# Second model, first layer: head pairs in the latent attention, its rotations moved ahead

## The chip, the cores and the metric

The kernel runs on one core of one Trainium2 chip. The metric is the device time of one execution in microseconds (us), the median of several runs; less is better.

## What is computed

The reference runs two models of two layers each on the same core: a hybrid mixer of four parts, and a second model that takes two token streams of 256 tokens (latent and context, 1024 channels) through a feed-forward part, a mixer and another feed-forward part in each layer, with a layer norm behind each. The change touches only the mixer of the second model's first layer, `even_mixer`. It runs a gated linear attention (GLA, four heads) and a latent attention (MLA, four heads: 128 channels without rotation, 64 rotated, values of 128), side by side on the same input:

```python
def apply_rope(x, cos, sin):
    x2 = x.reshape(*x.shape[:-1], -1, 2).astype(jnp.float32)
    x0, x1 = x2[..., 0], x2[..., 1]
    out = jnp.stack([x0 * cos - x1 * sin, x0 * sin + x1 * cos], axis=-1)
    return out.reshape(x.shape).astype(x.dtype)

def dense_attention(q, k, v, scale):
    ...
    def block(qi):
        s = jnp.einsum('bqhd,bkhd->bhqk', qi, k).astype(jnp.float32) * scale
        p = jax.nn.softmax(s, axis=-1).astype(v.dtype)
        return jnp.einsum('bhqk,bkhd->bqhd', p, v)
    ...

# inside even_mixer
    gla_l = gla_out(o_lf + flip(o_lb), r_l, gla_norm_g)
    q_l = jnp.concatenate([qn_l, apply_rope(qr_l, cos[None, :, None], sin[None, :, None])], axis=-1)
    kr_l_rot = apply_rope(kr_l, cos[None], sin[None])
    k_l = jnp.concatenate([kn_l, jnp.broadcast_to(kr_l_rot[:, :, None], rope_shape)], axis=-1)
    ...
    mla_l = dense_attention(q_l, k_all, v_all, MLA_SCALE).reshape(B, S, -1)
    yl = jnp.concatenate([gla_l, mla_l], axis=-1) @ w_out
    ...
    mla_c = dense_attention(q_c, k_c, v_c, MLA_SCALE).reshape(B, Tc, -1)
```

The latent queries see all 512 keys, the context queries the 256 context keys. Only the latent half of queries and keys is rotated; all four heads share one rotated key.

## The kernel before

Everything is written by hand: one instruction stream for each engine, with named semaphores (`on[...]`) between them. Weights come as slabs over SP's DMA queue into `raw`, a ring of four. ACT copies a slab to a rounded high part and DVE subtracts it from the slab to get the low part (`split_hi` L336, `split_lo` L340, called one slab ahead by `act_ahead` and `dve_ahead`); a product is then three matmuls, high by high, high by low and low by high (`dense` and `product` L375, `token_major` L417). The activations are split in the same way into `xh` and `xl`. An output bank pair is free again when `drained[...]` of its parity says so, and `last_pair` waits for both.

**The mixer's stages.** In `pe_even`, `act_even` and `dve_even`, slabs k = 0 to 8 of the input projection make the GLA queries and keys, the low-rank gate input and the rotated key (`LK`, chunk 0 and chunk 1), the compressed queries and keys `CQ`, the values and the gate `RS`. Beside them DVE and ACT work out the gates of the GLA's two directions. Then the GLA itself runs, and its output stands in `OA`. Seven small slabs follow (`uq` 0 to 2 and `ukv` 0 to 3): they make `QN` and `QR` (queries without and with rotation), `KN` (keys) and `VM` (values), token major. Beside these DVE normalises `OA` (L1347), multiplies it by `RS` (L1350), ACT copies it to `xh` (L1070) and DVE subtracts for `xl` (L1352).

**The rotation.** When the last slab is drained, PE permutes the latent half of `QR` (L1195) and of the key `LK` (L1196), two fp32 matmuls with a constant. DVE runs six operations (L1358 to L1363) that multiply by cosine and sine and add. `qk2_ready` then lets PE begin the attention.

**The attention.** `pe_attend`, `act_attend` and `dve_attend` go over `MLA_UNITS`: 16 units, one head and one block of 128 queries each. The 8 latent units have 512 keys, the 8 context units 256. For a unit PE computes the scores into one bank, as the sum of a product over 128 channels (`KN`, `QN`) and one over 64 (`LK`, `QR`), both L897; the 64 channels of an even head lie in partitions 0 to 63, those of an odd head in 64 to 127. DVE finds the negated maximum (L978) and scales it (L981), ACT takes the exponential with its sum (L941), DVE divides (L996, L999), PE transposes (L908), ACT copies back to `PTM` (L958) and PE multiplies by the values (L921). Two units are one head's output, which ACT and DVE split (L948, L989). Scores and probabilities have two buffers. PE's own order is what sets the pace:

```python
for u in range(len(units)):
    turn(u)
    if u + 2 < len(units):
        score(u + 2)
    if u:
        output(u - 1)
```

When all eight outputs are split, `pe_out` begins the output projection.

**The other layer's attention.** The second layer has a neighbourhood attention of 16 heads (`pe_pairs`, `act_pairs`, `dve_pairs`), which already goes by pairs of heads, one from each half of the partitions: four score banks, both scores of a pair next to each other (L1400, 64 channels each, 512 keys), then the transposes (L1409) and the products with the values (L1419). DVE has one operation more for each head there, a bias that is added to the scores.

Of the kernel before, what the change touches and what calls it, by code (L numbers as in the profile page):

```python
# [199 lines left out]
def build(nc, a):  # L200
# [8 lines left out]
    with ctx:  # L209
# [48 lines left out]
        def vcol(name, i, n=1):  # L258
# [28 lines left out]
        ml = phase([("c2_", [P, C2_N]), ("PR", [P, 2, 512]), ("K_", [P, 2, 2 * T]), ("LK_", [P, 2, 2 * T]),  # L287
                    ("PTM", [P, 2, 512]), ("V_", [P, 2, 512]), ("CQ_", [P, 4, 2 * T]),
# [202 lines left out]
        def segments(u):  # L491
# [8 lines left out]
                    soft_max exp_done p_ready pt_ready pt_copied pv_done o_taken pool_in pool_out var_ready root_done mixh_done x6_ready half_out x_centred row_ready row_out ln_all ln_sixth v_act cq_rstd cq_rows gq_rstd gq_rows qk_ready qb_ready n_max n_soft n_exp n_norm n_tr n_copy n_pv n_hi n_lo ctx_hi ctx_lo  # L500
                    mixl_done gates_e kc_ready rms_sum sc_ready mod_final xm_hi xm_lo x_scaled gate_act h_hi h_lo ln_sq ln_in
                    ln_sum z_out z_in z_ln ge_in ge_done kq_ready kd_t kdt_done att_out att_masked u_out s_ready og_out oa_done
                    gq_sum gq_sq mg_hi mg_ready cq_sq cq_sum cq_ready cq_hi cq_lo qk2_ready rm_out c2_in c3_in fmax fsoft fexp
                    fnorm ftr fcopy fpv fhi flo qkv_ready""".split()
# [67 lines left out]
        MLA_UNITS = [(h, blk, 0) for h in range(4) for blk in range(2)] + [(h, blk, 1) for h in range(4) for blk in range(2)]  # L572
# [307 lines left out]
        def unit_keys(units, u):  # L880
            return (0, 2 * T) if units[u][2] == 0 else (T, 2 * T)

        def groups(units, na):

            step = 4 if na else 2
            return {g * step + step - 1: g for g in range(len(units) // step)}

        def pe_attend(pe, units, na, f0, g0, q_ap, k_ap, v_ap, pr, ptm):

            def score(u):  # L890
                h, blk, ctx_ = units[u]
                k0, k1 = unit_keys(units, u)
                if f0 + u >= 2 and u >= 2:
                    pe.wait_ge(on["fexp"], f0 + u - 1)
                pairs = q_ap(h, ctx_ * T + blk * P, k0, k1)
                for n, (q, k) in enumerate(pairs):
                    mm = pe.matmul(PS[:, u % 2, 0:k1 - k0], q, k, start=n == 0, stop=n == len(pairs) - 1)  # L897
                mm.then_inc(on["fmax"], 1)
            score(0)
            score(1)  # L900

            def turn(u):
                k0, k1 = unit_keys(units, u)
                pe.wait_ge(on["fnorm"], f0 + u + 1)
                if u >= 2:
                    pe.wait_ge(on["fcopy"], f0 + u - 1)
                for kt in range((k1 - k0) // P):
                    mm = pe.transpose(PS[:, 2 + u % 2, kt * P:(kt + 1) * P], pr[:, u % 2, kt * P:(kt + 1) * P], ident)  # L908
                mm.then_inc(on["ftr"], 1)

            def output(u):
                h, blk, ctx_ = units[u]
                k0, k1 = unit_keys(units, u)
                pe.wait_ge(on["fcopy"], f0 + u + 1)
                g = u // (4 if na else 2)
                if g >= 2 and u % (4 if na else 2) == 0:
                    pe.wait_ge(on["flo"], g0 + g - 1)
                rows = slice((h % 2) * HD, (h % 2) * HD + HD) if na else slice(0, P)
                nk = (k1 - k0) // P
                for kt in range(nk):  # L920
                    mm = pe.matmul(PS[rows, 4 + g % 2, blk * P:(blk + 1) * P], v_ap(h, k0 // P + kt),  # L921
                                   ptm[:, u % 2, kt * P:(kt + 1) * P], start=kt == 0, stop=kt == nk - 1)
                mm.then_inc(on["fpv"], 1)
# [1482 lines left out]
```

## Time and profile before

| | |
|---|---|
| median of 3 runs | 2261.88 us (2260.73 to 2262.16) |
| the profiled execution: time, span | 2258.81 us, 2257.0 us |
| PE, DVE, ACT, POOL busy, share of the span | 94%, 62%, 33%, 6% |
| mean granted TensorE clock | 0.958 |
| PE, first matmul of the rotation | at 959.38 us |
| PE, first matmul of the attention | at 965.46 us |
| PE, first matmul of the output projection | at 1017.95 us |

Times are those of the span, which begins with the first instruction. The granted clock is 1 at 2.4 GHz and 0.5 at 1.2 GHz. An fp32 matmul stands in the trace as two records, so "x2" is one such matmul of the program, and the time from one row's start to the next row's start tells what it took.

### The profile page before, as it was taken

The numbers are of one execution on the slowest core, as the hardware profiler recorded it, in microseconds if no ns is written. First come the engines' busy times: TensorE is split into PE (matmuls) and PEld (weight loads), VectorE is DVE, ScalarE is ACT, GpSimd is POOL, SyncE is SP. The second block draws the span as 40 slices with busy tenths as digits, with TensorE's granted clock in tenths as the row PEclk, the third lists the DMA queues.
The fourth block names the chain that finished last, engine by engine and source line by source line (L and its number), as shares of the span: only waits on it lengthen the run. The fifth ranks groups of instructions, "written<-read, shape, count | busy, mean of one in ns | idle before, by whom it ended". The sixth has DMA issues, their size and how long they took to land. (4 is left out here: it accounts for less than half of the span.)

```text
span 2257.0 us, 28660 instructions
## 1 busy us (share of the span) xinstructions
PE 2113.5 (94%) x11984; PEld 1782.5 (79%) x11984; DVE 1392.5 (62%) x2005; ACT 745.8 (33%) x929; POOL 138.7 (6%) x127
## 2 busy tenths in 40 slices
PE   7979987999999899798999999899999989898997
PEld 6958966887887788647887887788888879778997
DVE  5775686586676556554676686555455455576555
ACT  3444345321121444233421222431122242355332
POOL 0400120000001100002000000100000200010001
PEclk9988988999999999889999999999999999998999
DMA  5553463455453310202355553242442333114552
GB/s 208 180 168 112 170 206 112 149 169 202 163 191 114 106 64 19 81 18 94 126 190 180 171 186 120 90 177 92 169 157 100 108 144 130 55 41 137 174 177 89
DMA packets 69209, 301.29 MB, mean 133 GB/s; under 512 B 6112, under 2 KB 24160, under 8 KB 49120
## 3 DMA queue, kind: packets, MB, share of 16 engines
q1 hardware_dynamic: 65712, 289.20, 37.2%
q10 hardware_dynamic: 3376, 10.37, 1.3%
q8 instruction: 89, 1.46, 0.3%
q14 instruction: 32, 0.26, 0.0%
HBM read 298.50 MB, written 1.05 MB: 133 GB/s over the span
## 5 line engine op out<-in xcount | busy, mean ns | idle before, releaser
L375 PE MATMUL PS<-xh,wh 128*128 128x512 f32 (+1 forms) x3740 | 1034.5, 351 | 23.6 <-DVE xl L2089 13.2
L375 PEld LDWEIGHTS PS<-xh,wh 128*128 128x128 f32 x3740 | 679.6, 190 | 119.3 <-issue 11.3
L375 PE MATMUL PS<-xl,wh 128*128 128x512 f32 (+1 forms) x2134 | 730.1, 342 | 0.0
L336 ACT ACTIVATE wh<-raw 128x2048 fp32r<-128x2048 f32 (+3 forms) x228 | 390.2, 1713 | 341.6 <-PE PS L375 238.7
L340 DVE TENSOR_TENSOR wh<-raw,wh 128x2048 fp32r<-128x2048 f32 (+3 forms) x188 | 388.4, 2066 | 131.6 <-ACT wh L336 131.2
L375 PEld LDWEIGHTS PS<-xl,wh 128*128 128x128 f32 x2134 | 407.9, 191 | 45.4
L375 PE MATMUL PS<-HH,wh 128*128 128x512 f32 (+1 forms) x1408 | 399.9, 368 | 6.6 <-DVE wh L340 6.6
L375 PEld LDWEIGHTS PS<-HH,wh 128*128 128x128 f32 x1408 | 253.7, 188 | 56.2 <-DVE wh L340 8.8
L832 DVE CUSTOM_DVE_ANT_0 NRM<-SQ,CBR 128x1024 f32<-128x1024 f32 x240 | 283.8, 1219 | 5.8
L375 PE MATMUL PS<-HL,wh 128*128 128x512 f32 (+1 forms) x704 | 258.5, 367 | 0.0
L774 ACT ACTIVATE SI<-PS 128x512 f32<-128x512 f32 (+1 forms) x88 | 48.1, 546 | 607.1 <-PE PS L375 575.4
L846 DVE TENSOR_TENSOR HF<-SI,PS 128x512 f32<-128x512 f32 (+1 forms) x88 | 54.6, 621 | 262.5 <-ACT SI L774 262.5
L661 DVE SCALAR_TENSOR_TENSOR X<-PS,mod,X 128x256 f32<-128x256 f32 x136 | 60.0, 479 | 154.3 <-PE PS L375 153.8
L375 PEld LDWEIGHTS PS<-HL,wh 128*128 128x128 f32 x704 | 132.6, 188 | 24.9
L375 PE MATMUL PS<-xh,rest 128*128 128x256 f32 x528 | 151.7, 287 | 0.0
L405 PE MATMUL PS<-xh,wh 128*128 128x512 f32 (+1 forms) x384 | 123.5, 403 | 26.4 <-DVE xl L628 26.4
L340 DVE TENSOR_TENSOR rest<-raw,wh 128x2048 fp32r<-128x2048 f32 (+2 forms) x40 | 89.4, 2241 | 38.4 <-ACT wh L336 37.8
L405 PEld LDWEIGHTS PS<-xh,wh 128*128 128x128 f32 x384 | 77.6, 209 | 43.8 <-issue 21.9
L689 POOL TENSOR_TENSOR NRM<-X 128x512 f32<-128x512 f32 (+1 forms) x6 | 6.7, 1113 | 1670.4 <-DVE X L661 1670.4
L375 PEld LDWEIGHTS PS<-xh,rest 128*128 128x128 f32 x528 | 103.8, 197 | 0.0
L678 ACT ACTIVATE SQ<-X 128x512 f32<-128x512 f32 (+2 forms) x42 | 25.7, 612 | 218.5 <-DVE X L661 218.5
L417 PE MATMUL PS<-wh,xh 128*128 128x256 f32 x400 | 75.6, 292 | 4.6 <-DVE wh L340 4.6
(322 smaller groups left out, 1935.6 us busy)
## 6 DMA issues: line engine op xcount, KB each, us to landing
raw<-ffi_dram SPq DMA_DIRECT2D x88, 1024.0 KB, 5.0
SQ<-adat_dram SPq DMA_DIRECT2D x120, 512.0 KB, 4.0
raw<-ffo_dram SPq DMA_DIRECT2D x64, 704.0 KB, 4.3
raw<-layer_dram SPq DMA_DIRECT2D x36, 1024.0 KB, 4.9
lent<-layer_dram SPq DMA_DIRECT2D x14, 1024.0 KB, 8.1
raw<-odd_dram SPq DMA_DIRECT2D x12, 1024.0 KB, 4.8
raw<-even_dram SPq DMA_DIRECT2D x9, 1024.0 KB, 4.9
raw<-eout_dram SPq DMA_DIRECT2D x4, 1024.0 KB, 4.8
```

The source lines that it names most:

```text
L336: act.activation(high(i)[:, 0:n], raw[:, i.slot, 0:n], ACT.Copy).then_inc(hi_done, 1)
L340: eng.tensor_tensor(low(i)[:, 0:n], raw[:, i.slot, 0:n], high(i)[:, 0:n].bitcast(F32), ALU.subtract).then_inc(lo_done[who], 1)
L375: m = pe.matmul(out, w[rows, o:o + P], x, start=n == 0 and j == 0, stop=n == len(tiles) - 1 and j == 2)
L405: m = pe.matmul(PS[:, 2 * j.par + c, 0:n], w[:, o:o + P], x[:, k, 0:n], start=k == 0 and g == 0, stop=k == KT - 1 and g == 2)
L417: m = pe.matmul(out, x[:, krow + k, tt * P:(tt + 1) * P], w[:, k * n:(k + 1) * n], start=k == 0 and j == 0, stop=k == kts - 1 and j == 2)
L661: mm = dve.scalar_tensor_tensor(out=xk, in0=PS[:, bank, br * T:(br + 1) * T], scalar=g, in1=xk, op0=ALU.mult, op1=ALU.add)
L678: act.activation(SQ[:, part, 0:n], X[:, part, 0:n], ACT.Square).then_inc(on["ln_sq"], 1)
L689: ins = pool.tensor_tensor(NRM[:, j, 0:n], src[:, 0, 0:n] if k == 1 else NRM[:, j, 0:n], src[:, k, 0:n], ALU.add)
L774: act.activation(SI[:, i.par, 0:n], PS[:, 2 * i.par, 0:n], ACT.Silu).then_inc(on["gate_act"], 1)
L832: mm = dve.tensor_tensor_reduce(out=NRM[:, 2 * br:2 * br + 2, :].rearrange("p a n -> p (a n)"), in0=ADA[:, n % CHUNK_RING, :], in1=CBR[:, ...
L846: dve.tensor_tensor(hf, SI[:, i.par, 0:n], PS[:, 2 * i.par + 1, 0:n], ALU.mult)\
```

## The change

**Head pairs.** `pe_mla`, `act_mla` and `dve_mla` take the place of the three functions of the attention. They go over 8 pairs: two heads, one block of 128 queries; four latent pairs with 512 keys, then four context pairs with 256. A pair has both products over 128 channels and then both over 64 channels, the latter from the two halves of the partitions and into two banks. Scores and probabilities have four buffers, and a pair of heads has one output bank, which ACT and DVE split in one operation each.

**Rotations.** The permutation of the key goes behind slab k = 3 of the input projection and its three DVE operations to k = 4. The permutation of the queries goes behind `ukv` slab 1, once DVE has normalised `OA` (new semaphore `gq_read`, since both use bank 4), and its three DVE operations come in slab k = 5 of the seven small ones, ahead of the splitting of the next slab.

**The rest of the GLA output.** Multiplying by `RS`, copying to `xh` and subtracting for `xl`, three operations of 2048 columns, become four of 512 columns each, put between the pairs.

```diff
-        ml = phase([("c2_", [P, C2_N]), ("PR", [P, 2, 512]), ("K_", [P, 2, 2 * T]), ("LK_", [P, 2, 2 * T]),
-                    ("PTM", [P, 2, 512]), ("V_", [P, 2, 512]), ("CQ_", [P, 4, 2 * T]),
+        ml = phase([("c2_", [P, C2_N]), ("PR", [P, 4, 512]), ("LK_", [P, 2, 2 * T]),
+                    ("PTM", [P, 4, 512]), ("CQ_", [P, 4, 2 * T]),
...
+        MLA_PAIRS = [(hp, blk, c) for c in range(2) for hp in range(2) for blk in range(2)]
...
+        def pe_mla(pe):
+            def scores(w):
...
+                if w >= 2:
+                    pe.wait_ge(on["m_exp"], 2 * w - 2)
+                for e in range(2):
+                    pe.matmul(PS[:, 2 * (w % 2) + e, 0:k1 - k0], ml["QN"][:, 2 * hp + e, q], ml["KN"][:, 2 * hp + e, k0:k1], start=True, stop=False)
+                for e in range(2):
+                    r = slice(e * HD, e * HD + HD)
+                    pe.matmul(PS[:, 2 * (w % 2) + e, 0:k1 - k0], ml["QR"][r, hp, q], ev["LK"][r, 1, k0:k1], start=False, stop=True)\
+                        .then_inc(on["m_max"], 1)
+            def turn(w):
...
+                for e in range(2):
+                    pe.wait_ge(on["m_norm"], 2 * w + e + 1)
+                    if w:
+                        pe.wait_ge(on["m_copy"], 2 * w + e - 1)
...
+            for w in range(len(MLA_PAIRS)):
+                turn(w)
+                if w + 2 < len(MLA_PAIRS):
+                    scores(w + 2)
+                if w:
+                    output(w - 1)
...
+        def act_mla(act):
...
+            for w in range(n):
+                for e in range(2):
+                    if w + 1 < n:
+                        exp(2 * w + 2 + e)
+                    copy(2 * w + e)
+                if 2 <= w < 6:
+                    act.wait_ge(on["mg_ready"], w - 1)
+                    act.activation(xh[:, w - 2, :], ev["OA"][:, w - 2, :], ACT.Copy).then_inc(on["mg_hi"], 1)
+                if w and w % 2 == 0:
+                    hi(w // 2 - 1)
...
+        def dve_mla(dve, ch):
...
+            for w in range(n):
+                for e in range(2):
+                    normal(2 * w + e)
+                    if w + 1 < n:
+                        maxima(2 * w + 2 + e)
+                if w < 4:
+                    dve.tensor_tensor(ev["OA"][:, w, :], ev["OA"][:, w, :], ev["RS"][:, w, :], ALU.mult).then_inc(on["mg_ready"], 1)
+                else:
+                    dve.wait_ge(on["mg_hi"], w - 3)
+                    dve.tensor_tensor(xl[:, w - 4, :], ev["OA"][:, w - 4, :], xh[:, w - 4, :].bitcast(F32), ALU.subtract)\
+                        .then_inc(on["mg_lo"], 1)
...
@@ pe_even, slab k == 3 of the input projection
                     gate_inputs(0)
+                    pe.matmul(PS[:, 7, 0:T], cst("permM"), ev["LK"][:, 1, 0:T], start=True, stop=True).then_inc(on["rk_out"], 1)
@@ pe_even, ukv
+                if k == 1:
+                    pe.wait_ge(on["gq_read"], 1)
+                    pe.matmul(PS[:, 4, :], cst("permM"), ml["QR"][:, :, 0:T], start=True, stop=True).then_inc(on["rm_out"], 1)
             last_pair(pe, Idx(START["ukv"] + 3))
-            pe.wait_ge(on["mg_ready"], 1)
-            pe.matmul(PS[:, 4, :], cst("permM"), ml["QR"][:, :, 0:T], start=True, stop=True)
-            pe.matmul(PS[:, 5, 0:T], cst("permM"), ev["LK"][:, 1, 0:T], start=True, stop=True).then_inc(on["rm_out"], 1)
             pe.wait_ge(on["qk2_ready"], 1)
...
-            pe.wait_ge(on["flo"], 8)
+            pe_mla(pe)
+            pe.wait_ge(on["m_lo"], 4)
+            pe.wait_ge(on["mg_lo"], 4)
             pe_out(pe, 1)
```

The moves on two engines, as lists of their instructions. First PE at the attention's first units, before. `KN`, `QN` is the product over 128 channels, `LK`, `QR` the one over 64, `const`, `PR` a transpose, `PTM`, `VM` the product with the values:

```order
L1195 MATMUL PS<-QR,const 128x512
L1196 MATMUL PS<-LK,const 128x256
L897 MATMUL PS<-KN,QN 128x512
L897 MATMUL PS<-LK,QR 128x512
L897 MATMUL PS<-KN,QN 128x512
L897 MATMUL PS<-LK,QR 128x512
L908 MATMUL PS<-const,PR 128x128 x4
```

The same place with the change:

```order
L891 MATMUL PS<-KN,QN 128x512 x2
L894 MATMUL PS<-LK,QR 128x512 x2
L891 MATMUL PS<-KN,QN 128x512 x2
L894 MATMUL PS<-LK,QR 128x512 x2
L904 MATMUL PS<-const,PR 128x128 x8
```

Both products of a kind now stand next to each other, with eight transposes behind them in place of four, and the permutations (L1195, L1196) are gone from this place.

DVE between the keys' second copy and the first maximum, before. `wh` is a slab's low part, `VM` the values' copy out of their banks, `c` the table of cosines and sines:

```order
L1332 COPY KN<-PS 128x1024
L1350 TENSOR_TENSOR OA<-OA,RS 128x2048
L340 TENSOR_TENSOR wh<-raw,wh 128x256
L1334 COPY VM<-PS 128x4x256
L340 TENSOR_TENSOR wh<-raw,wh 128x2048
L1334 COPY VM<-PS 128x4x256
L1352 TENSOR_TENSOR xl<-OA,xh 128x2048
L1358 TENSOR_TENSOR PR<-PS,c_94 128x512
L1359 TENSOR_TENSOR PR<-PS,c_94 128x256
L1360 TENSOR_TENSOR QR<-QR,c_94 128x2x256
L1361 TENSOR_TENSOR LK<-LK,c_94 128x256
L1362 TENSOR_TENSOR QR<-QR,PR 128x2x256
```

With the change:

```order
L1337 COPY KN<-PS 128x1024
L340 TENSOR_TENSOR wh<-raw,wh 128x256
L1339 COPY VM<-PS 128x4x256
L1358 TENSOR_TENSOR PR<-PS,c_94 128x512
L1359 TENSOR_TENSOR QR<-QR,c_94 128x2x256
L1360 TENSOR_TENSOR QR<-QR,PR 128x2x256
L340 TENSOR_TENSOR wh<-raw,wh 128x2048
L1339 COPY VM<-PS 128x4x256
L975 TENSOR_REDUCE tiny<-PS 128x1
```

The three operations on the queries now stand between the two copies to `VM`, ahead of the big slab's low part; those on `LK` and the two on `OA` are gone from here.

## Rows read from the trace of the kernel before

**Rows 1.** Windows, busy time by engine; the first line names the columns
```profile
core 0: us, PE busy (x) PEld busy (x) DVE busy (x) ACT busy (x) POOL busy (x), PEclk, DMA share, GB/s
818.00:842.00 24.00, 24.00 (x135) 20.11 (x134) 14.11 (x15) 11.60 (x8) 0.00 (x0) 1.00 0.08 23
921.00:926.00 5.00, 4.78 (x11) 3.81 (x12) 1.12 (x2) 2.64 (x2) 0.00 (x0) 0.50 0.02 3
950.00:965.00 15.00, 6.35 (x21) 4.09 (x19) 11.75 (x12) 4.99 (x3) 0.00 (x0) 0.51 0.57 205
965.00:981.00 16.00, 15.54 (x23) 5.02 (x23) 4.88 (x14) 3.31 (x8) 0.00 (x0) 0.50 0.00 0
983.50:997.30 13.80, 13.80 (x67) 7.74 (x66) 6.83 (x18) 5.66 (x15) 0.00 (x0) 1.00 0.00 0
1004.50:1012.20 7.70, 7.70 (x42) 5.05 (x41) 5.05 (x18) 3.91 (x14) 0.00 (x0) 1.00 0.02 3
```

**Rows 2.** Timeline of PE: start, us, line, tiles, count [idle before <-releaser]
```profile
948.80 0.50 PE L417 MATMUL PS<-wh,xh 128*128 128x256 f32 x2 [2.67 <-DVE wh L340]
...
959.38 2.05 PE L1195 MATMUL PS<-QR,const 128*128 128x512 f32 x2 [3.99 <-issue]
961.22 1.06 PE L1196 MATMUL PS<-LK,const 128*128 128x256 f32 x2
965.46 2.07 PE L897 MATMUL PS<-KN,QN 128*128 128x512 f32 x2 [3.17 <-DVE LK L1363]
```

**Rows 3.** Timeline, DVE, second gate, last projections and rotation
```profile
853.46 0.16 DVE L1277 TENSOR_SCALAR tiny<-PS 128x4 f32<-128x4 f32 x1 [6.90 <-PE PS L1115]
...
945.95 2.34 DVE L1347 SCALAR_TENSOR_TENSOR OA<-OA,vec,PS 128x2048 f32<-128x2048 f32 x1
...
949.80 2.28 DVE L1350 TENSOR_TENSOR OA<-OA,RS 128x2048 f32<-128x2048 f32 x1
...
955.86 2.29 DVE L340 TENSOR_TENSOR wh<-raw,wh 128x2048 fp32r<-128x2048 f32 x1 [2.31 <-ACT wh L336]
958.06 1.22 DVE L1334 COPY VM<-PS 128x1024 f32<-128x1024 f32 x1
```

**Rows 4.** Timeline, PE, one unit of 512 keys and the next one's start
```profile
983.48 1.02 PE L897 MATMUL PS<-KN,QN 128*128 128x512 f32 x2
984.43 1.12 PE L897 MATMUL PS<-LK,QR 64*128 64x512 f32 x2
985.49 1.16 PE L921 MATMUL PS<-PTM,VM 128*128 128x128 f32 x8
...
986.92 1.02 PE L897 MATMUL PS<-KN,QN 128*128 128x512 f32 x2
```

**Rows 5.** Timeline, PE, one unit of 256 keys and the next one's start
```profile
1006.47 0.60 PE L897 MATMUL PS<-KN,QN 128*128 128x256 f32 x2
1007.00 0.70 PE L897 MATMUL PS<-LK,QR 64*128 64x256 f32 x2
1007.62 0.71 PE L921 MATMUL PS<-PTM,VM 128*128 128x128 f32 x4
...
1008.39 0.60 PE L897 MATMUL PS<-KN,QN 128*128 128x256 f32 x2
```

**Rows 6.** Timeline, PE, attention end and first output matmul
```profile
1015.40 0.44 PE L908 MATMUL PS<-const,PR 128*128 128x128 f32 x2 [0.64 <-DVE PR L999]
...
1017.95 0.50 PE L375 MATMUL PS<-xh,wh 128*128 128x512 f32 x1 [0.93 <-DVE xl L989]
```

**Rows 7.** Timeline, PE, the other layer's attention, its first pairs
```profile
1954.01 1.11 PE L1409 MATMUL PS<-const,NP 128*128 128x128 f32 x4 [1.00 <-DVE NP L1477]
...
1958.97 0.66 PE L1409 MATMUL PS<-const,NP 128*128 128x128 f32 x4 [1.18 <-DVE NP L1477]
1959.55 1.13 PE L1400 MATMUL PS<-NK,NQ 64*128 64x512 f32 x4
1960.61 1.09 PE L1419 MATMUL PS<-NPT,NV 128*64 128x128 f32 x16
```

More of the change, by code:

```diff
@@ L877, in dve_ffn @@
             post_norm(dve, ch, m)
[L880 to L918, printed above, removed]
-                nk = (k1 - k0) // P
[L920 to L923, printed above, removed]
-            for u in range(len(units)):
-                turn(u)
-                if u + 2 < len(units):
-                    score(u + 2)
-                if u:
-                    output(u - 1)
-            output(len(units) - 1)
@@ new lines, in dve_mla, with maxima, normal @@
+        def dve_mla(dve, ch):
+            n = len(MLA_PAIRS)
+            def maxima(v):
+                k0, k1 = mla_keys(v // 2)
+                dve.wait_ge(on["m_max"], v + 1)
+                nm = tiny[:, v % 4:v % 4 + 1]
+                ch.after(dve.tensor_reduce(nm, PS[:, v % 4, 0:k1 - k0], AX, ALU.max, negate=True))
+                dve.tensor_scalar(nm, nm, MLA_SCALE, None, ALU.mult).then_inc(on["m_soft"], 1)
+            def normal(v):
+                k0, k1 = mla_keys(v // 2)
+                dve.wait_ge(on["m_exp"], v + 1)
+                r = tiny[:, 8 + v % 4:9 + v % 4]
+                ch.after(dve.reciprocal(r, tiny[:, 4 + v % 4:5 + v % 4]))
+                q = ml["PR"][:, v % 4, 0:k1 - k0]
+                dve.tensor_scalar(q, q, r, None, ALU.mult).then_inc(on["m_norm"], 1)
+            def lo(g):
+                hp, blk, c = MLA_PAIRS[2 * g]
+                dve.wait_ge(on["m_hi"], g + 1)
+                both, q = slice(4 + 2 * hp, 6 + 2 * hp), slice(c * T, (c + 1) * T)
+                dve.tensor_tensor(xl[:, both, q], PS[:, 6 + g % 2, :].rearrange("p (e t) -> p e t", e=2), xh[:, both, q].bitcast(F32),
+                                  ALU.subtract).then_inc(on["m_lo"], 1)
+            maxima(0)
+            maxima(1)
+            for w in range(n):
+                for e in range(2):
+                    normal(2 * w + e)
[7 more added lines that the diff above has]
+                        .then_inc(on["mg_lo"], 1)
+                if w >= 3 and w % 2:
+                    lo((w - 3) // 2)
+            lo(n // 2 - 1)
@@ L1067, in act_even @@
                     act_root(act, tiny[:, 104:120])
-                if k == 5:
-                    act.wait_ge(on["mg_ready"], 1)
-                    act.activation(xh[:, 0:4, :], ev["OA"][:, :, :], ACT.Copy).then_inc(on["mg_hi"], 1)
-            act_attend(act, MLA_UNITS, False, 0, 0, MLA_SCALE, ml["PR"], ml["PTM"], 4)
+            act_mla(act)
+            act.wait_ge(on["mg_lo"], 4)
             act.dma_start(CBR[:, :, :], a["cond"].rearrange("p (b n) -> p b n", b=2)).then_inc(cond_in, 16)
@@ L1274, in dve_even @@
                     gate_sums(0)
+                    dve.wait_ge(on["rk_out"], 1)
+                    rk = OA_[:, 0, 0:T]
+                    dve.tensor_tensor(rk, PS[:, 7, 0:T], cst("ropeM", c2, C2)[:, T:2 * T], ALU.mult)
+                    lk = ev["LK"][:, 1, 0:T]
+                    ch.after(dve.tensor_tensor(lk, lk, cst("ropeM", c2, C2)[:, 0:T], ALU.mult))
+                    ch.after(dve.tensor_tensor(lk, lk, rk, ALU.add))
                 if k == 5:
```

146 lines of the change are left out of this document (57 added, 89 removed).

## The prediction, made before the change was timed

> **What bounds the kernel now.** I read the page's busy shares first, then windows, then the timelines of PE and DVE around the latent attention. On the page PE is busy for 94% of the span, so a change pays where PE stands still, where it runs at the low clock, or where it does the same work in less time. The windows [rows 1] show three kinds of stretch. From 818 to 842 us PE is busy for 24.00 of 24.00 us at a granted clock of 1.00: there, whatever is added to PE costs its full time. From 950 to 965 PE is busy for 6.35 of 15.00 us: it waits for DVE and for ACT. From 965 to 981 it is busy for 15.54 of 16.00 us, but at 0.50, which is 1.2 GHz. The later stretches (983.5 to 997.3 and 1004.5 to 1012.2) are full at 1.00, with DVE busy for 6.83 of 13.80 and 5.05 of 7.70 us. So the attention is bound by PE, and what comes ahead of it by DVE.
>
> The seam [rows 2, 3]: PE finds its slab's low part at 948.80, works in two short bursts, and begins the rotation at 959.38, when DVE's second copy to VM (958.06, 1.22 us) is done. DVE's copy was late because ahead of it stood the multiplication of OA (949.80, 2.28 us) and the big slab's low part (955.86, 2.29 us), and this waited 2.31 us for ACT. The rotation then takes until 965.46, with PE idle for the last 3.17 us of it. From there to the output projection at 1017.95 [rows 6] it is 52.49 us.
>
> **The key's rotation, moved to slabs 3 and 4.** PE gets one fp32 matmul of 256 columns in the full stretch. The same shape took 0.53 us (1006.47 to 1007.00, [rows 5]), and nothing hides it: **+0.53**. DVE gets three operations of 256 columns, some 0.4 us each, so 1.2 us. DVE is busy for 14.11 of 24 us in that stretch [rows 1], and a little later it stands idle for 6.90 us until 853.46 [rows 3]. What is queued behind them (a slab's low part, a copy of values) comes 1.2 us later and PE asks for it after that idle time only: nothing. If the cover were gone, 1.2.
>
> **The start of the attention.** I follow DVE. Its normalisation of OA ends at 945.95 + 2.34 = 948.3, and only then may PE permute the queries. This falls in PE's pause before 948.80, but a matmul of 512 columns takes 0.95 to 1.06 us [rows 4], so the next slab begins near 949.4 instead of 948.8 and ends at 950.9. DVE copies KN until 949.9, makes the small slab's low part (0.4) with no multiplication of OA ahead of it, and copies VM from 951.0 to 952.2. Then come the query rotation's three operations, each of 512 columns and a quarter of the 2.28 us for 2048 or a little more, 1.9 together, to 954.1, the big slab's low part (2.2, and ACT has made the high part by then, since it no longer waits for OA), to 956.3, and the last copy (1.22), to 957.5. PE begins the scores at **957.6** instead of 965.46: 7.9 us earlier. Bounds: 956.5 if the permutation delays nothing, 960 if ACT's high part is late again as it is now.
>
> **PE's work in the attention.** At the full clock a unit of 512 keys takes 986.92 - 983.48 = 3.44 us: 0.95 for the product over 128 channels, 1.06 for the one over 64, the rest for the values and the transposes [rows 4]. A unit of 256 keys takes 1.92 us, with 0.53 and 0.62 [rows 5]. Eight of each are 42.9 us. In the other layer's attention two products over 64 channels with 512 keys, side by side in two halves of the partitions, take 1960.61 - 1959.55 = 1.06 us together [rows 7], which is what one takes here. So a pair with 512 keys should take 2 x 3.44 - 1.06 = 5.82 us and one with 256 keys 2 x 1.92 - 0.62 = 3.22, and four of each 36.2 us: **6.7 less**. The bounds are 0 (no overlap) and 6.7. The Trainium skill's page "TensorEngine Tiling (Array Packing)" (Key Properties) speaks against it: changing the tiling mode drains TensorE, and here each pair of 64-row products follows a 128-row product at once, in the middle of its sum. If that drain cost the overlap the sum would lose these 6.7 us. The row weighs against it: the other layer also changes over, from transposes to 64-row products, and its pair still takes 1.06.
>
> **The clock.** Now the clock is at 1.2 GHz until 981, 15.6 us after the attention began, although PE has no pause in them [rows 1]; that costs half, 7.8 us. What stood there was 128-row and single 64-row products by turns. Behind the pause before the query up-projection, dense 128-row matmuls ran at 0.50 only until 926 [rows 1], some 5.2 us. The new order begins with two 128-row products and a packed pair, no 64-row product alone, and I take the nearer row, 5.2 us, which costs 2.6: **5.2 less**. Bounds: 0 and 7.8 for the cost.
>
> **Pauses.** PE has scores of two pairs to do before it needs a result, 5.9 us at the full clock. In the other layer the second head's first transposes wait 1.00 us and those of the next pair 1.18 [rows 7], because DVE puts the next pair's maxima ahead of the second head's division; the same order stands here, and I add 2.3 us in all. Later DVE has about 3.4 us for a pair of 512 keys and 2.5 for one of 256, plus 0.6 for a quarter of OA's work, against 5.82 and 3.22 of PE: enough, barely so at the end. The end has now 0.64 and 0.93 of idle time [rows 6]; the splits are twice as wide, so 1.9 instead of 1.6.
>
> **The sum.** 957.6 + 36.2 + 2.6 + 2.3 + 1.9 = 1000.6, against 1017.95: 17.35 us less, and 0.53 is given back: 16.8. By its own time the profiled execution would go from 2258.81 to 2242.0. The median of the runs is 3.07 above it, so I forecast 2261.88 - 16.8 = **2245.1 us**. Nothing behind the output projection changes: its first slab is split in both orders before the attention, and its second just behind it.
>
> **The rivals.** First, the clock rises as late as now, 15.6 us after the start. For it: no pause kept it low before either. Against it: [rows 1], 921 to 926. It costs 5.2 us, of which 0.9 is hidden in the pauses: 2249.4. Second, the two 64-row products don't overlap, because they end sums that 128-row products began: 6.7 us more, 2251.8. Both together: 2256.1. Third, DVE becomes the bound: pairs with 256 keys and OA's quarters then come at DVE's pace, say 3.6 us instead of 3.22, and the start loses another microsecond: 1.5 + 1.0, 2247.6. Fourth, on the other side, the clock: with the two pauses at the start PE never gets 2.4 GHz back before the output projection. Then 36.2 us of work take 72.4, and the attention ends at 957.6 + 72.4 + 1.9 = 1031.9, which is 14.0 later than now: 2261.88 + 14.0 + 0.5 = 2276.4. It decides from about 39 us at the low clock behind the start (957.6 + 36.2 + 4.2 + 39/2 = 1017.5); now it is 15.6. That the change doesn't do what it says I rule out, for the lists of instructions show both the pairs and the moves.
>
> **How the numbers follow.** Forecast 0.60, late clock 0.17, no overlap 0.10, DVE 0.07, late clock and no overlap 0.03, clock low throughout 0.03. A measurement of this kernel can tell about 0.2%, 4.5 us, from no change, so faster means below 2257.4. All but the last two cases are well below it, and of the fifth I give 0.01 to faster and 0.02 to the same: faster 0.95, same 0.02, slower 0.03. The range goes from 2242.5 (the start at 956.5 and a clock that rises at once, less 1.1 and up to 2.6, not all of it) to 2252.0, which takes in the first three rivals and leaves the last two out.
>
> **What would show it.** Right: the first score product near 957.6 and the first output matmul near 1000.6; packed pairs of 1.06 and 0.62 us from one row's start to the next; 5.82 and 3.22 us for a pair; the clock at 1.00 from about 963; DVE without the 2.31 us wait for ACT. Wrong: 64-row pairs of 2.1 us, a clock of 0.50 past 970, PE waiting for DVE's division in pairs with 256 keys, or a pause of PE near 853 that the key's rotation made.

## The result, and the profile after

The changed kernel took **2238.34 us** in the median of 4 runs (2236.48 to 2244.32), against 2262.02 us for 4 runs of the kernel before: a ratio of 0.990, with an interval from 0.9879 to 0.992. The forecast was 2245.1 us, with a range from 2242.5 to 2252.0, so the sign was right and the gain, 23.7 us instead of 16.8, was outside the range. Later the changed kernel ran 17 times more: all 21 runs have a mean of 2240.4 us (standard error 0.7; 2236.1 to 2245.9), and 60 later runs of the kernel before have one of 2261.5 (0.3). One run of the kernel before, 2409.80 us at a mean clock of 0.82, is left out. So the gain that repeats is 21.0 us, and the other 2.7 us belong to the first group of runs. A number in brackets behind a mean or a difference is its standard error from here on.

The profiled execution took 2237.18 us. Its page begins so:

```profile
span 2235.4 us, 28654 instructions
PE 2093.8 (94%) x11984; PEld 1775.6 (79%) x11984; DVE 1390.7 (62%) x2007; ACT 745.9 (33%) x928; POOL 138.7 (6%) x127
```

PE is still busy for 94% of the span, and the shares of DVE (62%) and ACT (33%) are as they were. The windows below have the times of two windows of [rows 1]; the first line names the columns.

```profile
core 0: us, PE busy (x) PEld busy (x) DVE busy (x) ACT busy (x) POOL busy (x), PEclk, DMA share, GB/s
950.00:965.00 15.00, 10.27 (x28) 3.94 (x28) 9.22 (x18) 4.53 (x11) 0.00 (x0) 0.89 0.32 115
965.00:981.00 16.00, 15.03 (x95) 10.48 (x95) 10.90 (x33) 8.95 (x22) 0.00 (x0) 1.00 0.00 1
```

From 950 to 965 PE is now busy for 10.27 us at a mean clock of 0.89, where it had 6.35 at 0.51, and from 965 to 981 the clock is 1.00 instead of 0.50. The attention begins 11.7 us earlier in this profile, so the second window isn't the same work; counted from the first score, the clock is low for 3.1 us, where it was for 15.6.

The seam, PE's timeline (start, duration, engine, line, tiles, count, idle before and its releaser), the place of [rows 2]:

```profile
944.57 1.12 PE L1197 MATMUL PS<-QR,const 128*128 128x512 f32 x2 [2.21 <-DVE OA L1352]
945.13 0.80 PE L417 MATMUL PS<-wh,xh 128*128 128x256 f32 x2
...
953.75 3.48 PE L891 MATMUL PS<-KN,QN 128*128 128x512 f32 x4 [5.19 <-DVE VM L1339]
957.17 1.13 PE L894 MATMUL PS<-LK,QR 64*128 64x512 f32 x4
958.23 1.98 PE L891 MATMUL PS<-KN,QN 128*128 128x512 f32 x4
960.14 1.13 PE L894 MATMUL PS<-LK,QR 64*128 64x512 f32 x4
961.20 0.66 PE L904 MATMUL PS<-const,PR 128*128 128x128 f32 x4
962.83 0.66 PE L904 MATMUL PS<-const,PR 128*128 128x128 f32 x4 [0.97 <-DVE PR L984]
...
967.82 0.66 PE L904 MATMUL PS<-const,PR 128*128 128x128 f32 x4 [0.97 <-DVE PR L984]
968.31 1.88 PE L891 MATMUL PS<-KN,QN 128*128 128x512 f32 x4
970.12 1.13 PE L894 MATMUL PS<-LK,QR 64*128 64x512 f32 x4
971.18 2.05 PE L917 MATMUL PS<-PTM,VM 128*128 128x128 f32 x16
973.07 1.04 PE L904 MATMUL PS<-const,PR 128*128 128x128 f32 x8
973.94 1.03 PE L891 MATMUL PS<-KN,QN 128*128 128x256 f32 x4
...
975.54 2.05 PE L917 MATMUL PS<-PTM,VM 128*128 128x128 f32 x16
```

The permutation of the queries (L1197) waits for DVE's normalisation of OA and fills PE's pause, as forecast. The first score comes at 953.75 instead of 965.46; 7.94 us of that are the seam's, the rest lies ahead of it. Two products over 128 channels and two over 64 take 961.20 - 958.23 = 2.97 us for the second pair and 971.18 - 968.31 = 2.87 for a later one; with 256 keys they take 975.54 - 973.94 = 1.60. In these rows a transpose counts once, the other products over fp32 twice. The second head's first transposes wait 0.97 us in each of the first two pairs. DVE there, the place of [rows 3]:

```profile
942.18 2.34 DVE L1352 SCALAR_TENSOR_TENSOR OA<-OA,vec,PS 128x2048 f32<-128x2048 f32 x1
...
947.17 1.23 DVE L1339 COPY VM<-PS 128x1024 f32<-128x1024 f32 x1 [0.85 <-PE PS L417]
948.31 0.68 DVE L1358 TENSOR_TENSOR PR<-PS,c 128x512 f32<-128x512 f32 x1
...
950.23 2.29 DVE L340 TENSOR_TENSOR wh<-raw,wh 128x2048 fp32r<-128x2048 f32 x1
952.43 1.22 DVE L1339 COPY VM<-PS 128x1024 f32<-128x1024 f32 x1
958.39 0.69 DVE L975 TENSOR_REDUCE tiny<-PS 128x1 f32<-128x512 f32 x1 [4.74 <-PE PS L894]
```

The big slab's low part (950.23) no longer waits for ACT, and behind the last copy to VM DVE stands idle for 4.74 us. The end, the place of [rows 6]:

```profile
990.53 0.90 PE L904 MATMUL PS<-const,PR 128*128 128x128 f32 x4 [0.25 <-DVE PR L984]
991.27 1.95 PE L917 MATMUL PS<-PTM,VM 128*128 128x128 f32 x16
994.63 0.50 PE L375 MATMUL PS<-xh,wh 128*128 128x512 f32 x1 [1.41 <-DVE xl L990]
```

From the first score to the first output matmul it is 994.63 - 953.75 = 40.88 us, where it was 52.49.

### The profile page after: what moved, and what is told of

Its sections match the earlier page's. It is cut to its first block and busy times, and to the rows that moved or that the text cites. A ratio compares the mean times of both kernels' runs of the same rounds, so it can differ in the third digit from the quotient of the medians.

```text
span 2235.4 us, 28654 instructions
## 1 busy us (share of the span) xinstructions
PE 2093.8 (94%) x11984; PEld 1775.6 (79%) x11984; DVE 1390.7 (62%) x2007; ACT 745.9 (33%) x928; POOL 138.7 (6%) x127
## 5 line engine op out<-in xcount | busy, mean ns | idle before, releaser
L375 PE MATMUL PS<-xl,wh 128*128 128x512 f32 (+1 forms) x2134 | 730.4, 342 | 0.0
L375 PEld LDWEIGHTS PS<-HL,wh 128*128 128x128 f32 x704 | 132.5, 188 | 24.6
L405 PE MATMUL PS<-xl,wh 128*128 128x512 f32 (+1 forms) x192 | 76.3, 397 | 0.0
```

The costliest lines, as they stand in the source:

```text
L375: m = pe.matmul(out, w[rows, o:o + P], x, start=n == 0 and j == 0, stop=n == len(tiles) - 1 and j == 2)
L405: m = pe.matmul(PS[:, 2 * j.par + c, 0:n], w[:, o:o + P], x[:, k, 0:n], start=k == 0 and g == 0, stop=k == KT - 1 and g == 2)
```

## The experiments

In every profile three distances can be read, and they separate what the median mixes. **Ahead**: from DVE's copy of LK (slab 2) to the normalisation of OA. **Seam**: from that normalisation to the first score. **Attention**: from the first score to the first matmul of the output projection. "Low" is how long of the attention passed before the clock returned to 1.00. Times in us. The last column has the number of runs of that kernel and their mean; the distances are from one profile each, and the lines below a kernel are its further profiles.

```
                ahead   seam    attention  low   runs (mean)
before          136.0   19.51   52.49      15.6  60 (2261.5)
 more           134.4   19.51   52.52      15.7
                137.8   19.52   52.74      16.1
delay_slab3     134.9   19.50   52.50      15.6  12 (2262.2)
key_only        134.8   17.65   50.18      10.6  11 (2258.3)
rotations_only  137.2   13.44   52.45      15.5   9 (2254.9)
units_packed    136.1   19.51   47.87       5.4   9 (2257.5)
pairs_only      137.9   19.51   41.88       6.0   4 (2252.3)
alternate       134.0   11.57   54.71      20.8   5 (2252.0)
key_late        136.0   13.25   41.64       4.7  10 (2243.9)
 more           135.2   13.25   41.96       5.4
after           132.5   11.57   40.88       3.1  21 (2240.4)
 more           132.4   11.58   40.90       3.1
                132.5   11.57   40.83       3.0
                138.9   11.57   41.15       3.7
                137.3   11.57   41.14       3.6
                137.2   11.57   41.13       3.6
split_later     137.3    9.36   42.19       5.9   6 (2238.7)
best            134.8    9.37   35.32       0     9 (2235.7)
 more           138.9    9.36   38.07       5.8
```

One line sums up the clock: in the seven profiles in which every 64-row product stands alone it stayed low for 10.6 to 20.8 us of the attention, in the thirteen in which such products stand side by side for 0 to 6.0 us.

### The pairs alone

The changed kernel with both rotations and the three operations on OA back in their old places (`pairs_only`):

```diff
-                if k == 1:
-                    pe.wait_ge(on["gq_read"], 1)
-                    pe.matmul(PS[:, 4, :], cst("permM"), ml["QR"][:, :, 0:T], start=True, stop=True).then_inc(on["rm_out"], 1)
             last_pair(pe, Idx(START["ukv"] + 3))
+            pe.wait_ge(on["mg_ready"], 1)
+            pe.matmul(PS[:, 4, :], cst("permM"), ml["QR"][:, :, 0:T], start=True, stop=True)
+            pe.matmul(PS[:, 5, 0:T], cst("permM"), ev["LK"][:, 1, 0:T], start=True, stop=True).then_inc(on["rm_out"], 1)
             pe.wait_ge(on["qk2_ready"], 1)
             pe_mla(pe)
```

> The head pairs with their four buffers, but the rotations and the rest of the GLA output where they stood before the change. Theory A (the pairs are worth their overlap and a clock that rises within some 5 us): the attention's first matmul stays near 965.5 us, the stretch from there to the output projection falls from 52.5 us to 41 or 42, and the kernel takes about 2251. Theory B (the clock rises late whatever the order of the products, and was early in the changed kernel only because of what went before): the stretch is 46 to 47 us and the kernel takes about 2256.

Measured: 2252.36 us (2251.06 to 2253.45), ratio to before 0.9957 (0.9941 to 0.9974). The seam is that of before to a hundredth, 19.51 us, and the attention takes 41.88. The whole kernel is 9.2 us (0.6) below the mean of before. Its PE timeline shows where the clock rises:

```profile
966.39 3.78 PE L891 MATMUL PS<-KN,QN 128*128 128x512 f32 x4 [3.17 <-DVE LK L1353]
970.10 2.08 PE L894 MATMUL PS<-LK,QR 64*128 64x512 f32 x4
972.11 2.08 PE L891 MATMUL PS<-KN,QN 128*128 128x512 f32 x4
974.12 1.13 PE L894 MATMUL PS<-LK,QR 64*128 64x512 f32 x4
975.18 0.66 PE L904 MATMUL PS<-const,PR 128*128 128x128 f32 x4
```

The first packed pair takes 972.11 - 970.10 = 2.01 us at 1.2 GHz, the second 975.18 - 974.12 = 1.06 at 2.4. The pairs are worth 10.6 us of attention behind the old seam too, near the 11.6 that they have behind the new one: theory A.

### The rotations alone

The kernel before with both rotations moved, its units kept (`rotations_only`); the edit is the part of the change outside `pe_mla`, `act_mla` and `dve_mla`, with the multiplication by RS left in slab 4 and the subtraction for `xl` behind the seven slabs.

> The 16 units of before, with the two rotations moved as in the change; the three operations on the rest of the GLA output stay whole and where they were, and only the last of them now lies beside the first scores. Theory A: the first matmul of the attention comes 3 to 5 us earlier (two DVE operations of 2.3 us remain ahead of it), the stretch to the output projection stays at 52 to 53 us with 15 us of it at 1.2 GHz, and the kernel takes 2257 to 2260. Theory B: the stretch falls by up to 6 us too, since the pause ahead of it is shorter, and the kernel takes about 2252.

Measured: 2256.52 us (2245.80 to 2259.95), ratio 0.9967 (0.9953 to 0.9981). The seam is 6.1 us shorter, the attention 52.45 us: as long as before, with 15.5 us at the low clock, though the seam ahead of it was shorter. So the shorter seam alone doesn't bring the clock back sooner. The shortening of the seam came out larger than expected (3 to 5 us):

```profile
957.68 2.29 DVE L340 TENSOR_TENSOR wh<-raw,wh 128x2048 fp32r<-128x2048 f32 x1 [0.39 <-ACT wh L336]
```

DVE's wait for ACT ahead of the big slab's low part is 0.39 us instead of 2.31, for the three operations on the queries lie in it. The first score stands 13.44 us behind the start of the normalisation, where the first matmul of the rotation stood before (959.38 - 945.95 = 13.43).

### No two 64-row products next to each other

```diff
                 for e in range(2):
                     pe.matmul(PS[:, 2 * (w % 2) + e, 0:k1 - k0], ml["QN"][:, 2 * hp + e, q], ml["KN"][:, 2 * hp + e, k0:k1], start=True, stop=False)
-                for e in range(2):
                     r = slice(e * HD, e * HD + HD)
```

> The changed kernel with one edit: the product over 64 channels of a head follows its own product over 128 channels, so two 64-row products are never neighbours. Theory A: the overlap goes (6.7 us) and the clock stays at 1.2 GHz for 12 to 16 us behind the start (another 4 to 6 us): 2248 to 2251. Theory B: only the overlap goes: about 2245.

Measured: 2251.83 us (2247.93 to 2256.21), ratio 0.9956 (0.994 to 0.9972). One edit to the order of four matmuls gives back 13.8 us of the attention, and 11.6 us (1.6) of the mean. PE's timeline, at the start and at the full clock:

```profile
958.34 2.04 PE L891 MATMUL PS<-KN,QN 128*128 128x512 f32 x2 [5.18 <-DVE VM L1338]
960.31 2.07 PE L893 MATMUL PS<-LK,QR 64*128 64x512 f32 x2
962.31 2.07 PE L891 MATMUL PS<-KN,QN 128*128 128x512 f32 x2
...
982.60 1.02 PE L891 MATMUL PS<-KN,QN 128*128 128x512 f32 x2
983.55 1.12 PE L893 MATMUL PS<-LK,QR 64*128 64x512 f32 x2
984.60 1.13 PE L891 MATMUL PS<-KN,QN 128*128 128x512 f32 x2
985.66 1.12 PE L893 MATMUL PS<-LK,QR 64*128 64x512 f32 x2
986.71 2.05 PE L916 MATMUL PS<-PTM,VM 128*128 128x128 f32 x16
```

Every product takes 2.0 us at the low clock, and at the full clock four take 986.71 - 982.60 = 4.11 us, against 2.87 in the changed kernel. So packing is worth 1.24 us for a pair of 512 keys, more than the 1.06 of the forecast: a 128-row product between two 64-row ones takes 985.66 - 984.60 = 1.06 us, one behind transposes and ahead of a 64-row product 983.55 - 982.60 = 0.95, and two next to each other take 970.12 - 968.31 = 1.81 together. The windows show the clock of the stretch from 965 to 981, here 0.56:

```profile
965.00:981.00 16.00, 16.00 (x25) 5.19 (x24) 6.07 (x17) 3.73 (x9) 0.00 (x0) 0.56 0.00 1
```

20.8 us at the low clock instead of 3.1 cost 8.9 us, and four times 1.24 plus four times 0.81 (2.41 against 1.60 us with 256 keys) are 8.2, together 17.1. Of these 13.8 are seen: of the 2.2 us of pauses in the changed kernel only 0.19 are left here, and the rows behind them aren't lengthened, which is about the rest. That is theory A, whose clock stays low even longer than its 12 to 16 us, and whose 2251 us the median passes by 0.8. Theory B's 2245 us lies outside the interval (2248.2 to 2255.4).

### The units of before, with the array's other half filled

This is the sharpest of them: it adds work and is faster. L901 is the added product.

```diff
                     mm = pe.matmul(PS[:, u % 2, 0:k1 - k0], q, k, start=n == 0, stop=n == len(pairs) - 1)
                 mm.then_inc(on["fmax"], 1)
+                r = slice((1 - h % 2) * HD, (1 - h % 2) * HD + HD)
+                q0 = ctx_ * T + blk * P
+                pe.matmul(PS[:, 7 - h % 2, 0:k1 - k0], ml["QR"][r, h // 2, q0:q0 + P], ev["LK"][r, 1, k0:k1], start=True, stop=True)
```

> The kernel before with one matmul more in each unit: the same 64-row product from the other half of the partitions, into a bank that nobody reads, right behind the real one. The work that counts is the same, and the array's second half is filled. Theory A: the added product costs nothing at the full clock (it overlaps), and the clock rises within 4 to 8 us of the attention's start instead of 15.6, so the kernel gets faster by 3 to 5 us, 2257 to 2259. Theory B: no gain, 2262 or, if nothing overlaps, up to 16 x 1 us more, 2275.

Measured: 2257.77 us (2254.48 to 2259.80), ratio 0.9981 (0.9971 to 0.9991); the mean is 4.0 us (0.8) below that of before:

```profile
968.15 2.08 PE L897 MATMUL PS<-KN,QN 128*128 128x512 f32 x2 [3.18 <-DVE LK L1366]
970.15 1.22 PE L897 MATMUL PS<-LK,QR 64*128 64x512 f32 x1
970.16 1.22 PE L901 MATMUL PS<-LK,QR 64*128 64x512 f32 x1
...
978.03 1.02 PE L897 MATMUL PS<-KN,QN 128*128 128x512 f32 x2
978.98 0.69 PE L897 MATMUL PS<-LK,QR 64*128 64x512 f32 x1
978.99 0.69 PE L901 MATMUL PS<-LK,QR 64*128 64x512 f32 x1
...
981.47 1.02 PE L897 MATMUL PS<-KN,QN 128*128 128x512 f32 x2
```

Both products start within 0.01 us of each other, and a unit takes 981.47 - 978.03 = 3.44 us, as before, so the addition costs nothing. The clock rises 5.4 us after the first score instead of 15.6. The attention is 4.6 us shorter, close to half of those 10.2 us. Nothing else was changed, so what kept the clock down before was that the 64-row products stood alone. That the changes between the two kinds of product kept it down is excluded: there are as many of them as before. Whether the clock answers to how full the array is or to how much work passes through it per time, no run here tells apart.

### The key's rotation, and what the clock does ahead of the attention

Three kernels, one of them in two groups of runs, and further groups and single profiles of the two main kernels went to a question that the first profile raised: the distance ahead was 132.5 us in it and 136.0 before, although the change adds a matmul there. `key_only` is the kernel before with only the key's rotation moved; `key_late` the changed kernel with it next to the query's; `delay_slab3` the kernel before with an unused matmul more at slab 3:

```diff
                     gate_inputs(0)
+                    pe.matmul(PS[:, 7, 0:T], cst("permM"), ev["LK"][:, 1, 0:T], start=True, stop=True)
```

> The kernel before with the key's rotation alone moved to slabs 3 and 4, the query's left at the end. Removed at the end: one matmul of 256 columns at the low clock and three small DVE operations, some 1.2 us of DVE and 1 us of PE in the seam; added: 0.53 us of PE. Theory A: 2260 to 2262, and the position of DVE's normalisation of OA moves by 0.5 us and by clock chance. Theory C: it comes 3 to 4 us earlier, with a shorter low stretch behind 850 us: 2256 to 2258.

> The changed kernel with the key's rotation next to the query's (PE behind ukv slab 1, DVE in slab 5). Given back: 0.53 us of PE at slab 3. Added ahead of the attention: three DVE operations of 256 columns, 1.2 us, and one matmul. Theory A: within 1.5 us of the changed kernel, on the slow side. Theory C: 3 to 4 us slower than the changed kernel.

> The kernel before with one matmul of 256 columns more behind slab 3 of the input projection, whose result nobody reads; nothing is moved. Theory A (PE is bound there and the clock's drops are chance): +0.53, 2261 to 2263. Theory C (a PE shift ahead of the low-activity matmuls near 850 us makes the clock drop for less time in most runs): 2257 to 2260.

> The key's rotation late, once more, for more runs beside the changed kernel on the same chip. Theory A: within 1.5 us of the changed kernel's mean. Theory C: 3 to 5 us above it, as in the first five runs.

Measured: `key_only` 2258.31 us (2251.74 to 2263.20), ratio 0.9989 (0.9979 to 1.0000); `delay_slab3` 2263.96 us (2254.40 to 2266.89), ratio 1.0003 (0.999 to 1.0015); `key_late` 2243.97 us (2240.82 to 2245.78), ratio 0.9925 (0.9912 to 0.9938), and again 2243.50 (2241.62 to 2246.65), ratio 0.9919 (0.9905 to 0.9933). The added matmul alone moves the mean by +0.7 (1.1). The traces size it better: from DVE's copy of LK to PE's first matmul at L417 it is 24.13 to 24.15 us in the profiles with the matmul at slab 3 (833.93 - 809.79 in `delay_slab3`), and 23.69 or 23.70 in those without (833.63 - 809.93 before), so it costs 0.44 us. Theory C's 2257 to 2260 for `delay_slab3` didn't come: a shift at slab 3 doesn't make the clock drop less.

`key_only` came out just below theory A's 2260 to 2262, 3.2 us (1.2) under the mean of before. Its profile has 1.9 us less in the seam and 2.3 less in the attention, where the clock was low for 10.6 us instead of 15.6; ahead it has 134.8, within the 134.4 to 137.8 of the kernel before. Why the clock came back 5 us sooner there, with all its 64-row products alone, isn't shown; it says how far the low stretch can move without packing.

The late place costs 3.5 us (1.0) against the changed kernel, which is theory C's number and more than theory A's 1.5. 1.7 of them are seen in the seam and 0.8 in the attention, and 0.4 come back at slab 3; the remaining 1.4 are not told from nothing.

> The changed kernel once more, unchanged, to see how far its runs spread and how much of its gain belongs to one profile. Theory A (the gain is the attention's: 11 to 12 us less in it and 8 us ahead of it, and what the clock does before the attention varies from run to run by chance): median 2238 to 2243, runs from 2234 to 2246, and in its profile the attention takes 41 to 42 us. Theory C (moving the key's rotation makes PE's clock drop less before the attention, in every run): the same median, and the low stretch behind 850 us is 3.4 us long again.

> The changed kernel for the third time, for the same comparison. Both theories: median 2237 to 2243; with key_late_2 it settles whether the place of the key's rotation is worth more than the 0.5 us by which its own operations move.

> The changed kernel, one more profile. Theory A (chance of the start): in one of the two profiles the low-clock time between 840 and 940 us differs from 6.8 us, towards 10 to 17. Theory D (it belongs to the change): 6.8 us again in both.

> The kernel before, one more profile. Theory A: the low-clock time between 840 and 940 us lies anywhere from 7 to 20 us (17.0 in the first profile). Theory D: 13 to 20 us. In both the attention takes 51 to 53 us with the clock low for 12 to 16 us of it.

Measured: 2238.76 us (2236.06 to 2244.26) and 2240.24 us (2237.03 to 2245.33), and single runs of 2243.56 and 2245.87 for the changed kernel (the latter is `after_look_b`), 2260.76 and 2262.60 for the one before. The windows from 840 to 940 us, of `after_look_b` and of `after_third`:

```profile
840.00:940.00 100.00, 93.73 (x757) 84.21 (x756) 62.95 (x80) 36.88 (x34) 0.00 (x0) 0.91 0.05 14
```

```profile
840.00:940.00 100.00, 93.73 (x779) 83.86 (x779) 62.57 (x81) 34.80 (x34) 0.00 (x0) 0.97 0.09 28
```

PE is busy for the same 93.73 us in both, with a mean clock of 0.91 and of 0.97. So the same program shows either, the slow one in the profiles of 2243.56, 2245.87 and 2245.56 (`after_fourth`), the quick one in those of 2236.06, 2237.03 and 2237.18, and the distance ahead follows it: 137.2 to 138.9 against 132.4 to 132.5. It varies from run to run, and theory D, by which the changed kernel always takes the quick course, falls. The kernel before gave 134.4, 136.0 and 137.8. Why a run takes the one or the other course isn't shown by these records. Nor is it excluded that the change makes the quick one more frequent: it stands in three of the changed kernel's six profiles and in none of the fourteen of the other kernels.

### A version that goes further

`split_later` moves one DVE operation of the changed kernel, and `best` adds two edits more:

```diff
                 i = Idx(START["uq"] + k)
-                dve_ahead(dve, i)
+                if k < 6:
+                    dve_ahead(dve, i)
...
+            dve_ahead(dve, Idx(START["uq"] + 6))
             dve.wait_ge(on["gq_read"], 1)
             dve_mla(dve, ch)
...
+                if w < 2:
+                    normal(2 * w)
+                    normal(2 * w + 1)
                 for e in range(2):
-                    normal(2 * w + e)
+                    if w >= 2:
+                        normal(2 * w + e)
...
-            pe.wait_ge(on["m_lo"], 4)
+            pe.wait_ge(on["m_lo"], 3)
             pe.wait_ge(on["mg_lo"], 4)
...
+                if late is not None and n == late[2]:
+                    pe.wait_ge(late[0], late[1])
```

> The changed kernel with one DVE operation moved: the low part of the output projection's first slab (2.2 us) comes behind the last copy to VM instead of ahead of it. PE waits for that copy before it begins the scores, and DVE stands idle for 4.7 us behind it. Theory A (DVE's chain sets the start): the first score comes 2.2 us earlier, and the kernel takes 2.2 us less than the changed kernel, 2236. Rival (the start is set by something else, or the clock takes it back): no difference.

> The changed kernel with three edits: the low part of the output projection's first slab behind the last copy to VM (2.2 us of PE's start, measured in the profile of split_later); for the first two pairs DVE divides for both heads before it looks for the next maxima (two pauses of PE of 0.97 us); and PE begins the output projection with chunks 0 to 5 and waits for the last two heads' split only ahead of chunk 6 (1.4 us of idle time). Theory A: 5.5 us less than the changed kernel from slab uq 0 on, so 2234 in the median, 2230 to 2240 over its runs. Rival (the clock takes it back): the profile shows the 5.5 us, the median doesn't.

> The version with three edits (first slab's low part behind the last copy to VM, both heads' division first in the first two pairs, output projection begun before the last split), a second time. Theory A: its mean lies 4 to 7 us below that of the changed kernel on the same chip. Rival (the clock takes it back): within 2 us of it.

> The changed kernel beside it: a mean of 2239 to 2242 in both theories, with runs from 2236 to 2246.

Measured: `split_later` 2239.51 us (2232.78 to 2243.17), ratio to before 0.9902 (0.9886 to 0.9917); `best` 2237.98 us (2228.47 to 2239.29), ratio 0.9897 (0.9882 to 0.9912), and in the second group 2235.89 us (2230.51 to 2238.60), ratio 0.9883 (0.9864 to 0.9901), beside 2239.15 us (2236.99 to 2245.56), ratio 0.9901 (0.9885 to 0.9917), for the changed kernel. Nine runs of `best` have a mean of 2235.7 (1.3), 4.7 us below the 21 of the changed kernel, with a standard error of 1.5: it is very probably the fastest, though the intervals of the two groups still overlap. Its start:

```profile
952.37 1.96 PE L893 MATMUL PS<-KN,QN 128*128 128x512 f32 x4 [2.98 <-DVE VM L1347]
954.25 1.13 PE L896 MATMUL PS<-LK,QR 64*128 64x512 f32 x4
955.31 1.99 PE L893 MATMUL PS<-KN,QN 128*128 128x512 f32 x4
957.22 1.13 PE L896 MATMUL PS<-LK,QR 64*128 64x512 f32 x4
958.28 1.11 PE L906 MATMUL PS<-const,PR 128*128 128x128 f32 x8
959.23 1.88 PE L893 MATMUL PS<-KN,QN 128*128 128x512 f32 x4
```

The seam is 2.2 us shorter (9.37), as expected, and the two pauses of 0.97 us are gone: eight transposes stand in one row at 958.28. The attention took 35.32 us in this profile, in which the clock never fell there, and 998.23 - 960.16 = 38.07 us in the second one, in which it did. In that one seam and attention together are 47.4 us, against 52.7 in the changed kernel's profile of the same group (`after_fourth`): 5.3 of the 5.5 us expected.

`split_later` alone had the shorter seam too (9.36), but its mean is only 1.7 us (1.9) below the changed kernel's, so its worth isn't shown by the runs. Its profile says where part of it went: the scores begin 2.2 us earlier, the clock comes back no earlier (15.3 us behind the start of the normalisation, 15.2 in `after_fourth`), so 5.9 us of the attention are at the low clock, and it takes 42.19 us where the three profiles of the changed kernel with as slow a course ahead have 41.1. So the clock takes back about half.

## Why the prediction was off

**The seam: right.** The first score was forecast 7.9 us earlier through DVE's chain. The seam fell from 19.51 to 11.57 us, 7.94, in all profiles of the changed kernel. The permutation in PE's pause and the missing wait for ACT stand in the timeline as they were worked out.

**The key's rotation: right in kind.** Forecast +0.53 us, measured +0.44 in every profile that has it. The three DVE operations cost PE nothing, as forecast: in the changed kernel's profile DVE is still idle for 3.36 us of the old 6.90 when PE's result comes, and PE has no pause from 838 to 860.

**PE's work: right in kind, gain sized too small.** 36.2 us were forecast. At its steady pace a pair of 512 keys takes 2.87 for the scores, 1.89 for the values and 0.87 for the transposes: 5.63 instead of 5.82; one with 256 keys takes 1.60 for the scores and half of the rest, 2.98 instead of 3.22. Four of each are 34.4, and that is 8.5 us less than the 42.9 of before, where the forecast had 6.7 as the most that could be had; the rows behind pauses and at the ends are longer by about 1.3 in all (the transposes 0.66 + 0.49 there instead of 0.87). The rival without overlap is excluded by these rows. The Trainium skill's page "TensorEngine Tiling (Array Packing)" (Key Properties) says that a change of the tiling mode drains TensorE. This trace agrees with a price for each change: a 128-row product takes 1.81 - 0.95 = 0.86 us between two like ones, 0.95 with one change and 1.06 with two, so a change costs some 0.10 us. The pairs change half as often, two changes fewer in each pair: 0.20 us, about what a pair is shorter than forecast (0.19 and 0.24). The forecast kept all the changes of the single units, and in it the page stood against the pairs, where here it speaks for them.

**The clock: right in kind, gain sized too small.** I took 5.2 us at 1.2 GHz behind the start, from a row with dense matmuls. It was 3.0 to 3.7 us in six profiles, and part of the size is luck: the low stretch of 3.4 to 6.8 us begins 0.3 to 3.3 us ahead of the first score, in PE's pause, where it costs nothing (in `after` the clock falls at 953.4 and the score comes at 953.75). The reason I gave in passing, that single 64-row products stood in the old stretch, is what `units_packed` and `alternate` show to be the cause; the late-clock rival and the one with a clock that stays low are excluded.

**Pauses.** 2.3 us forecast, 0.97 + 0.97 + 0.25 = 2.2 measured; at the end 1.9 forecast, 1.41 measured. Together 34.4 + 1.3 + 1.6 (for 3.1 us at the low clock) + 2.2 + 1.4 = 40.9 us, where I had 36.2 + 2.6 + 2.3 + 1.9 = 43.0.

**The step that failed** is the sum for the attention, and the range that was built on it. The costs in the sum were put too high: PE's work at 36.2 us where it took 35.7, the clock at 2.6 where it took 1.6, the end at 1.9 where it took 1.4, the pauses by 0.1. That is 2.1 us, and it alone would have given 2242.8 us, just inside the range.

The rest of the miss lies in what the range took as fixed. Seam, attention and slab 3 make 7.9 + 11.6 - 0.4 = 19.1 us of the 21.0 that repeat. The other 1.9 aren't seen in the profiles: all that lies outside seam and attention takes 2186.8 us in the mean of three profiles before and 2186.5 in the mean of six with the change, slab 3 included, with single profiles from 2182 to 2191. They aren't told apart from the clock's varying course (the two means have a standard error of 0.8 together), and they stay open. The range took the stretches that the change doesn't touch as fixed, although one profile can't tell that; runs of the changed kernel spread over 10 us. Its lower end also held back part of its own bounds: 2245.1 - 1.1 - 2.6 would be 2241.4, and 2242.5 was written. Even 2241.4 lies above the 2238.34 measured and the 2240.4 that repeats, since no bound was set for a pair cheaper than 5.82 us, nor for the runs' own spread.

## What to carry over

Matmuls that contract over 64 rows belong next to each other in opposite halves of the array: here they overlapped (1.06 us for two of 512 columns, as long as for one), cost fewer changes of kind, and the clock came back sooner. Read the clock's row for every stretch in which PE is busy without a pause and still slow; the order of its products may be the reason. And when a term of a forecast is a clock that changes, one profile is one draw: take several, or widen the range by what they may differ.

## What the runs showed of the hardware

Three things I had not expected. Adding a 64-row product in the array's idle half made the same program faster by 0.2% (0.9981, 0.9971 to 0.9991), and the clock rose 10 us sooner in its profile. With every product alone (`alternate`) PE was busy for 16.00 of 16.00 us at a clock of 0.56: full busy time doesn't mean the full clock. And the same program, started again, spends 160 us of its span at 1.2 GHz in one run and 188 in another (the profiles of 2236.06 and 2245.87 us). The 28 us more would cost 14 if PE had been busy in all of them; the two runs differ by 9.8.
